# A fused two-block transformer kernel: the feed-forward layers open with four feature blocks side by side instead of two

## What is computed

```
u = causal_dwconv(h @ w_up, conv_w)          # 3 taps over the tokens
gate, up = split(u, [2816])                  # 2816 features each
return (gelu(gate) * up) @ w_down
```

## Time and profile before

| | |
|---|---|
| median of 3 runs | 1261.51 us |
| the profiled execution | 1262.73 us, its span 1260.7 us (2.0 us lie outside the span) |
| TensorE matmul busy | 1195.9 us, 95% of the span |
| TensorE weight load busy | 1121.5 us, 89% |
| VectorE busy | 864.8 us, 69% |
| ScalarE busy | 709.8 us, 56% |
| GpSimd busy | 61.8 us, 5% |
| memory read | 158.28 MB, 126 GB/s over the span |

### The profile page before, as it was taken

How to read it: one execution, slowest core, us unless ns; L and a number is a source line. 1 busy time by engine, 2 the same in 40 slices (tenths; PEclk the granted TensorE clock), 3 DMA queues, 4 the chain that set the end, 5 groups by cost and what they waited for, 6 DMA issues and landing times.

```text
span 1260.7 us, 27818 instructions
## 1 busy us (share of the span) xinstructions
PE 1195.9 (95%) x10201; PEld 1121.5 (89%) x10201; DVE 864.8 (69%) x1691; ACT 709.8 (56%) x1478; POOL 61.8 (5%) x69
## 2 busy tenths in 40 slices
PE   5999998999999899988999899999999999899996
PEld 5888877999999799977998799999988999899995
DVE  5888865777754577766444577885466786778874
ACT  6677664666644467654225566665455655655543
POOL 0000000121100000002000011210000000000000
PEclk9999998999999999988998999999999999999998
DMA  7433314455555255530000436566634343444431
GB/s 260 125 128 102 126 60 130 129 171 171 169 172 159 77 188 150 163 111 2 2 2 2 134 101 187 179 178 180 179 114 148 120 148 120 134 145 139 133 117 35
DMA packets 49977, 160.35 MB, mean 127 GB/s; under 512 B 5488, under 2 KB 8432, under 8 KB 49776
## 3 DMA queue, kind: packets, MB, share of 16 engines
q1 hardware_dynamic: 49904, 159.35, 40.9%
HBM read 158.28 MB, written 1.05 MB: 126 GB/s over the span
## 4 chain that ended last, share of the span: by engine, by line
PE 86%; DVE 7%; ACT 5%; issue 2%; DMA 0%; SPq 0%; ACTq 0%; DVEq 0%
PE banks L365 23%; PE banks L367 21%; PE banks L366 21%; PE banks L1475 2%; PE banks L1483 2%; ACT w_hi L346 2%; PE banks L902 2%; PE banks L438 1%; DVE w_lo L351 1%; PE banks L882 1%; PE banks L867 1%; DVE m L518 1%; PE banks L1491 1%; PE banks L485 1%; DVE t_sin L1131 1%
## 5 line engine op out<-in xcount | busy, mean ns | idle before, releaser
L351 DVE TENSOR_TENSOR w_lo<-raw,w_hi 128x1024 fp32r<-128x1024 f32 (+5 forms) x332 | 370.4, 1122 | 195.4 <-ACT w_hi L346 194.4
L365 PE MATMUL banks<-x_hi,w_hi 128*128 128x272 f32 (+2 forms) x1624 | 476.8, 294 | 8.0 <-DVE x_lo L498 3.9
L367 PE MATMUL banks<-x_hi,w_lo 128*128 128x272 f32 (+2 forms) x1624 | 464.2, 286 | 0.0
L366 PE MATMUL banks<-x_lo,w_hi 128*128 128x272 f32 (+2 forms) x1624 | 464.0, 286 | 0.0
L346 ACT ACTIVATE w_hi<-raw 128x1024 fp32r<-128x1024 f32 (+5 forms) x332 | 314.4, 955 | 92.2 <-PE banks L367 87.4
L365 PEld LDWEIGHTS banks<-x_hi,w_hi 128*128 128x128 f32 x1624 | 307.2, 189 | 25.6 <-issue 15.3
L366 PEld LDWEIGHTS banks<-x_lo,w_hi 128*128 128x128 f32 x1624 | 307.9, 190 | 0.1
L367 PEld LDWEIGHTS banks<-x_hi,w_lo 128*128 128x128 f32 x1624 | 307.3, 189 | 0.0
L365 PE MATMUL banks<-hid_hi,w_hi 128*128 128x272 f32 (+1 forms) x352 | 101.3, 288 | 0.0
L367 PE MATMUL banks<-hid_hi,w_lo 128*128 128x272 f32 (+1 forms) x352 | 100.3, 285 | 0.0
L366 PE MATMUL banks<-hid_lo,w_hi 128*128 128x272 f32 (+1 forms) x352 | 99.9, 284 | 0.0
(11 more groups left out here) (288 smaller groups left out, 1820.7 us busy)
## 6 DMA issues: line engine op xcount, KB each, us to landing
raw<-w_up SPq DMA_DIRECT2D x88, 512.0 KB, 4.4
raw<-w_attn SPq DMA_DIRECT2D x32, 512.0 KB, 4.6
raw<-w_dn SPq DMA_DIRECT2D x32, 512.0 KB, 4.0
raw<-w_moba SPq DMA_DIRECT2D x32, 512.0 KB, 3.9
raw<-w_down SPq DMA_DIRECT2D x32, 384.0 KB, 3.2
raw<-w_down SPq DMA_DIRECT2D x32, 320.0 KB, 3.2
raw<-w_mla SPq DMA_DIRECT2D x16, 384.0 KB, 3.2
raw<-w_attn_out SPq DMA_DIRECT2D x8, 512.0 KB, 4.2
```

Of the source, the lines that this page charges most:

```text
L351: nc.vector.tensor_tensor(w_lo[:, q, 0:wd], raw[:, q, 0:wd], w_hi[:, q, 0:wd].bitcast(F32), ALU.subtract).then_inc(lo_done, 1)
L365: nc.tensor.matmul(dst, hi, src[0][:, k, c0:c1], start=first, stop=False)
L366: nc.tensor.matmul(dst, hi, src[1][:, k, c0:c1], start=False, stop=False)
L367: return nc.tensor.matmul(dst, lo, src[0][:, k, c0:c1], start=False, stop=last)
```

## The change

`two_products` is renamed `side_by_side`; its body is the same and takes any number of destinations. In the feed-forward layers it is called with all four banks: for each k the products of blocks 0, 1, 2 and 3. The separate call for blocks 2 and 3 goes away. In the latents and the third attention only the name changes; both still pass two banks.

```
-        def two_products(pe, name, dsts, cols, x_base):
+        def side_by_side(pe, name, dsts, cols, x_base):
             for k in range(KT):
                 pe.wait_ge(x_ready, x_base + k + 1)
                 for q, dst in enumerate(dsts):
                     if k == 0:
                         weights_here(pe, name, 0, q)
                     mm = product(dst, q, k * P, x_op, k, cols, k == 0, k == KT - 1)
                     if k == KT - 1:
                         mm.then_inc(chunk_used, 1)
...
             if f:
                 pe.wait_ge(conv_done, FT * f)
-            two_products(pe, name, (bank[0][:, c0:c1], bank[1][:, c0:c1]), cols, X_BASE[f"pre{2 * f + 1}"])
-            unit(0, (1,))
+            side_by_side(pe, name, [bank[q][:, c0:c1] for q in range(4)], cols, X_BASE[f"pre{2 * f + 1}"])
             with pe.Fori(1, FT // 2) as u:
                 unit(u)
...
-                    two_products(pe, "w_moba", (bank[0][:, 0:SEQ], bank[1][:, 0:SEQ]), (META, T), X_BASE["ln1"])
+                    side_by_side(pe, "w_moba", (bank[0][:, 0:SEQ], bank[1][:, 0:SEQ]), (META, T), X_BASE["ln1"])
...
-            two_products(pe, "w_latent", (bank[0][:, c0:c1], bank[1][:, c0:c1]), (c0, c1), X_BASE["post3"])
+            side_by_side(pe, "w_latent", (bank[0][:, c0:c1], bank[1][:, c0:c1]), (c0, c1), X_BASE["post3"])
```

## The result

| | before | with the change |
|---|---|---|
| median | 1261.51 us (5 runs, 1257.89 to 1262.75) | 1268.98 us (5 runs, 1264.25 to 1272.65) |
| ratio | | 1.0061, 95% interval 1.0042 to 1.0080 |
| profiled execution, its span | 1262.73, 1260.7 | 1264.25, 1262.2 |

The change costs 7.5 us by the medians, 5.3 to 10.1 by the interval. The forecast was 8.6 us. When the same kernel was timed again beside other experiments it came to 1267.15 against 1261.03 us, ratio 1.0049 (1.0036 to 1.0062). One execution of the kernel before in that second set, 1661.59 us at a mean granted clock of 0.651, was in a slower state and is left out of the ratio.

A forecast was written before the change was run, and what follows sets the result against it. TensorE was taken to bound the kernel (86% of the chain of waits). Stalls and clock, 3.09 + 2.93 + 2 x 1.3 = 8.6 us, put the median at 1261.5 + 8.6 = 1270.1 us, range 1265.5 to 1275.5.

The forecast's parts named there:

- Part 1: Latents and third attention: only the helper's name changes, two banks passed as before; cost 0.
- Part 2: Start of both feed-forward layers: four blocks fill TensorE's waits for x; gain 0 in the first, 0.12 us in the second.
- Part 3: Start of unit 1: cover shrinks from 52 matmuls to 10, so TensorE stalls 3.09 us in the first layer, 2.93 in the second.
- What is late next: Unit 1 after the stall: later chunks and loads are covered, chunk 2's low part by only one microsecond.
- Part 4: Behind each layer's stall TensorE's granted clock falls, costing 1.3 us per layer.
- (a): Both layers: stalls come, but the clock does not fall or falls in one only; 6.0 to 7.3 us, 1268; chance 22%.
- (b): Unit 1: the r = 1 chain is late too, or the low clock lasts longer; 11 to 14 us, 1274; chance 12%.
- (c): Not slower: later work moves against the clock's low stretches and repays the loss; about 1261 us; chance 3%.
- (d): Side-by-side start lacks x after all and four blocks fill it; at most 0.2 us per layer, changes no chance.
- (e): First 96 matmuls: rotating over four banks itself lowers the clock, 12 us more per layer, in all 1294; chance 1%.

The follow-up runs named there:

- four_filled: The change plus 22 filler matmuls on an unread bank between unit 0 and unit 1; 1264.36 us against 1261.03 for the kernel before, ratio 1.0033.
- slow_x_four: The change plus two spare VectorE operations per tile of x in both feed-forward layers; 1269.33 us against 1261.03 for the kernel before, ratio 1.0072.
- four_then_two: The change with four blocks side by side only for tiles 0 and 1, two for tiles 2 to 7; 1261.67 us against 1260.41 before, ratio 1.0008.

## Why the prediction was right

- **Part 1** (latents, third attention: only a name). Nothing in the runs speaks against it. From the second layer's first matmul on `hid` to the last group of matmuls, a stretch that holds the latents and the third attention, the two kernels take the same time to 0.03 us (1253.44 - 854.52 = 398.92 and 1254.90 - 856.01 = 398.89).
- **Part 2** (gain 0 and 0.12 us). The claim was that TensorE already runs behind x, and it does: in the first layer the matmuls' pace is the same with two blocks and with four. The 0.12 is below what the totals can show, but the traces have it: in the second layer the first 96 matmuls take 11.53 us from the first start to the last in the kernel before, and 11.41 in four_filled and in slow_x_four, all at a granted clock of 1.00.
- **Part 3** (the stall). Forecast 3.09 and, gain left out, 3.05; measured 3.01 and 2.97. The difference is one term: the matmul follows the low part by 0.05 us (232.06 - 232.01), where the earlier trace rows had given 0.14. The tap 0.32 us behind the matmul (0.33 by the rows) and the chain of 3.89 both held.
- **What is late next**: nothing, as forecast. Chunk 2's low part was ready at 235.91 + 1.22 = 237.13, and TensorE wanted it 48 matmuls after 232.06, at 238.06: cover 0.9 us, forecast 0.9.
- **Part 4** (clock, 1.3 us per layer). The size was right (1.3 to 1.4), the frequency too high: six waits of ten instead of all. This is the weak term of the forecast: it rested on one wait of two, and a longer wait was taken to make the fall certain. With 0.6 x 2 x 1.3 = 1.6 in place of 2.6 the sum is 5.98 - 0.12 + 1.6 = 7.5 us. That this is the difference of the medians to the digit is luck, since the same kernel timed again gave 6.2. The Trainium skill's rule ("TensorE: Matmul & The Clock Gate", Part 1), that idleness drops the clock and sustained work restores it, agrees with six waits of ten here and with both filled gaps; in the other four the clock stayed at 1.00.
- **Rivals.** (a), the stalls without the fall of the clock or with it in one layer only, is what the change's own profile did (second layer only), and slow_x_four in both layers without any fall. Its 1268 us is even nearer to the measured 1268.98 than the forecast's 1270.1, and its 6.0 to 7.3 us holds the 6.2 of the second measurement. The times don't tell the forecast from (a); what is certain is the part that both share, the two stalls. (b) did not occur: no second wait stood in unit 1. (c) is the most instructive: the profiled execution really had 6.4 us less elsewhere, 4.7 of them between the layers with the mean clock at 0.97 instead of 0.95. But that is scatter of single executions, and the median keeps the loss. (d) was rightly dismissed (0.12 us), and (e) is refuted by four_then_two and by 92 matmuls in 11.25 us.

## What to carry to other kernels

Computing several blocks side by side while an input arrives fills idle time only up to the width at which one tile's work equals one tile's arrival (here 6 matmuls, 0.75 us, against 0.74). Every block beyond that lets more results end together and takes cover from the chain that empties them and prepares the next weights: compare that chain (4.26 us here) with the work left after the first block ends. If both are wanted, go wide for the first tiles only; here that lost nothing, and it gained nothing either.

## What the runs showed that I had not expected

- The unchanged code between the two layers took 372.41 us in one execution and 377.14 in another, with a mean granted clock of 0.97 and 0.95: one profile's span is no measure of a change of under 1% here.
- The spare one-input VectorE operation on 128x272 costs 0.21 us of pace, though its row says 0.29 and the two-input ones beside it 0.43 to 0.49; a row's duration is not its price in a full queue.
- Idle time within the x phase costs twice, once as idle time and once in the clock: with x at 2.65 us per tile the two-block kernel's stretch from 221 to 238 us ran at a granted clock of 0.52, the four-block kernel's at 0.86.
- Equal waits fell out differently from one execution to the next: behind the wait of 1.69 us the clock fell in 5 profiles of 14, behind those of 2.8 us at unit 1 in 6 of 10. A forecast should put a chance on such a term and not the full price.
